# Two hybrid layers before two attention-and-experts layers on one core: small loads after the first weights, both attentions' turns side by side, four banks for the sections between

## The chip, the cores and the metric

The kernel runs on one NeuronCore of a Trainium2 chip. The metric is the device time of one execution in microseconds (us). All data is float32. Five engines work side by side: TensorE (PE, its weight loads are PEld), VectorE (DVE), ScalarE (ACT), GpSimd (POOL) and SyncE (SP), which here only issues loads. They wait for each other through semaphores, and each runs its own instructions in order.

## The reference

256 tokens of width 1024 go through two blocks of two layers each. The change touches the first block alone. One of its layers computes

```
h = rmsnorm(x);  p = h @ w_in                      # 1024 -> 3488, split in 15 parts
q = rmsnorm(cq) @ w_uq ; kv = rmsnorm(ckv) @ w_ukv # latent attention ("mla"), 4 heads of 96
q = rope(rmsnorm(q)); k = [rmsnorm(k_nope), rope(rmsnorm(kr))]
o_a = causal_attention(q, k, v_a)
o_b = c_b * short_conv(c_c * c_h)                  # 3 taps
o_c = sg_u * (tril(sg_w) @ layernorm(sg_v) + sg_b)
qd, kd = rope(rmsnorm(mq)), rope(rmsnorm(mk))      # second attention ("moba"), 4 heads of 64
o_d = causal_attention(qd, kd, mv)                 # 256 tokens are one block: plain causal
x = x + [o_a silu(g_a), o_b silu(g_b), o_c silu(g_c), o_d silu(g_d)] @ w_out
```

The second block has two layers, each an attention (neighbourhood, then grouped) and 32 experts of which each token uses two; all experts' weights are read. A vector `c` gives shifts, scales and gates of the second block through `ada_w` (1024 x 6144 for each layer).

## The kernel before

Everything stands in one program with one block per engine; the order of the work is written out by hand, engine by engine, and a result's place is found by name: `begin(b, name)` on TensorE waits until PSUM bank b is free (`drained`), `end` signals `filled`, and the engine that copies the result out signals `drained`. There are eight banks of 128 x 512.

**Weights.** They come in pieces of 1024 x 512 (2 MB), or 1024 x 416 for `cq`, into a ring of five slots, all issued by SyncE in the order of `LOADS` (line 60). A piece waits until the one that held its slot is used up. For the first layer the order is cq, qk, v, ada, s, a, ada, b, ada, g, ... Before `qk`, SyncE waits (in the first layer only) for all small loads `in` and `lay0`.

**Small loads** are issued by GpSimd at its start: five under the name `in` (positions, two gains, `c`, and 128 x 704 of constants), then `layer_loads(0)` (six, named `lay0`: gains, taps, `w_uq`, `w_ukv`, `sg_w`), then ten named `in2`. Behind them on GpSimd's queue stand the reciprocal roots that the norms wait for (line 2171): `xrs`, then, after a wait for `lay0` and four selections on `sg_w`, `rs6`, `rs8`, `rs12`, `srs`.

**A layer of the first block** (`first_layer`, on each engine its own). TensorE: 16 turns of x into columns (`xT`); the two products `cq`; the section `qk` of the first token tile; `cqT`, `ckT` turns; `qk` of the second tile; the products `q` and `kv`; then, by calls of `fill()`, the sections v0, v1, a sum `tot` of an `ada` vector, s0. A section is 16 products of 128 x 256 (32 passes in the trace). It waits for `mla` and turns the first attention's queries and keys (`hT`, 16 turns, banks 0 to 3); then section s1; then it waits for `moba` and turns the second attention's (`dT`, 8 turns, banks 0 and 1); then `attend` runs four groups of scores, softmax, turns and values, with a `fill()` (a0, a1, ...) in each round. The banks of the fills are dealt out in turn from `fill_bank`: 7 and 6 up to the attention, then 7, 2, 3. In the second layer the fill of qk1 has a `tot` too.

VectorE's fills are emptied by `settle()` in the order of `MIX_SIDE`, ScalarE's in the order of `FILL`. VectorE scales and rotates the first attention's queries and keys (tells `mla`), empties `tot` and v1, copies half of `hT`, then waits for `sq12` (ScalarE's squares of the second attention's, which ScalarE makes after `mla` and after its copies of `hT`), sums them, gets `rs12` from GpSimd, scales and rotates (tells `moba`), copies half of `dT`, and goes into `attend`.

In the names of the rows `bk` is a PSUM bank, `ring` the weight ring, `AR` the arena with nearly all activations, `st` the small statistics, `diag` the scratch of the `ada` sums. Line 425 is a turn, 429 a product, 637 a group's scores, 1009 a VectorE tensor_tensor, 2297 SyncE's load.

## Time and profile before

| | us |
|---|---|
| median of 3 runs | 1616.68 (1615.48 to 1617.62) |
| the profiled execution | 1619.63 |
| its span on the core | 1617.9 |
| TensorE matmuls busy in it | 1407.1 (87%) |
| VectorE busy | 568.5 (35%) |
| ScalarE busy | 219.3 (14%) |
| GpSimd busy | 87.9 (5%) |

The first block takes about the first 345 us of the span, the neighbourhood attention the stretch up to about 530, its experts up to about 985, and the second attention and its experts the rest. In the experts' stretches the DMA engines are nine tenths busy in every slice; in the first 345 us they are not. "PEclk" is the share of TensorE's full clock that was granted; it has two levels, 0.5 (1.2 GHz) and 1.0 (2.4 GHz). Idle time in square brackets names what ended it.

### The profile page before, as it was taken

How to read it: one execution, taken by the hardware profiler on the slowest of the kernel's cores; microseconds unless marked ns; L12 is line 12 of the kernel's file. 1: busy time of each engine (PE TensorE's matmuls, PEld its weight loads, DVE VectorE, ACT ScalarE, POOL GpSimd, SP SyncE). 2: the span in 40 equal slices, each digit the busy share in tenths (PEclk: the TensorE clock that was granted, in tenths of full speed). 3: DMA queues.
4: the chain of work that ended last, by engine and by line, in shares of the span. 5: the costliest groups of instructions: out<-in, count | busy, mean ns of one | idle time of the engine just before them, and what ended most of it. 6: DMA issues, size and time to landing. Idle time of an engine off the chain costs nothing.

```text
span 1617.9 us, 28390 instructions
## 1 busy us (share of the span) xinstructions
PE 1407.1 (87%) x12800; PEld 893.9 (55%) x12800; DVE 568.5 (35%) x1230; ACT 219.3 (14%) x578; POOL 87.9 (5%) x95
## 2 busy tenths in 40 slices
PE   6989998999899898897897887878899888887895
PEld 3776467758787554363464443447554544544542
DVE  2586557655765111011111105593411111111113
ACT  2131113202242000000000001342200000000000
POOL 3110102000002100000000000100300000000000
PEclk9999999999998999899899998989899988999999
DMA  9545853686757899999999999345799999999995
GB/s 341 199 155 200 297 204 121 240 290 235 270 198 286 350 426 426 427 426 428 428 425 427 427 387 332 117 156 217 295 426 426 426 427 427 426 427 428 426 418 203
DMA packets 96858, 533.33 MB, mean 330 GB/s; under 512 B 5185, under 2 KB 7425, under 8 KB 73169
## 3 DMA queue, kind: packets, MB, share of 16 engines
q1 hardware_dynamic: 92992, 519.40, 79.7%
q0 software_dynamic: 3728, 11.95, 2.1%
q8 instruction: 105, 1.72, 0.4%
q14 instruction: 33, 0.26, 0.0%
HBM read 530.28 MB, written 1.05 MB: 328 GB/s over the span
## 4 chain that ended last, share of the span: by engine, by line
PE 62%; DMA 25%; DVE 7%; ACT 2%; issue 1%; SPq 1%; POOL 0%; DVEq 0%; ACTq 0%
PE bk L429 24%; DMA AR<-in_moe_w_down 24%; PE bk L890 17%; PE bk L924 8%; PE bk L608 3%; PE bk L934 3%; PE bk L425 3%; DVE AR L1009 3%; ACT AR L1815 2%; PE bk L637 1%; PE bk L652 1%; SPq L2297 1%; DMA ring<-in_w_in 1%; DVE mpart L1017 1%; DMA ring<-in_ada_w 1%
## 5 line engine op out<-in xcount | busy, mean ns | idle before, releaser
L890 PE MATMUL bk<-ring,AR 128*32 128x128 f32 x5120 | 307.8, 409 | 3.8 <-DVE AR L1014 3.8
L890 PEld LDWEIGHTS bk<-ring,AR 128*32 128x32 f32 x5120 | 192.6, 127 | 102.3 <-DVE AR L1014 4.8
L429 PE MATMUL bk<-ring,AR 128*128 128x256 f32 (+2 forms) x736 | 216.3, 452 | 18.6 <-DMA ring<-in_w_in 7.1
L1009 DVE TENSOR_TENSOR AR<-bk,AR 128x128 f32<-128x128 f32 (+2 forms) x106 | 41.2, 389 | 531.6 <-ACT AR L1815 467.7
L1815 ACT ACTIVATE AR<-bk 128x512 f32<-128x512 f32 (+4 forms) x178 | 71.8, 422 | 1070.2 <-PE bk L890 789.2
L924 PE MATMUL bk<-ring,AR 128*32 128x512 f32 x656 | 161.8, 706 | 38.9 <-DMA ring<-in_moe_w_down 38.9
L429 PEld LDWEIGHTS bk<-ring,AR 128*128 128x128 f32 x736 | 142.8, 197 | 87.0 <-issue 55.5
L924 PE MATMUL bk<-AR 128*32 128x512 f32 x368 | 146.5, 704 | 48.9 <-DMA AR<-in_moe_w_down 48.1
L890 PE MATMUL bk<-AR 128*32 128x128 f32 x3072 | 187.4, 410 | 0.4 <-DMA AR<-in_moe_w_up 0.4
L429 PE MATMUL bk<-AR,ring 128*128 128x256 f32 (+1 forms) x832 | 175.4, 371 | 6.9 <-DVE diag L1009 5.5
L429 PEld LDWEIGHTS bk<-AR,ring 128*128 128x128 f32 x832 | 150.8, 194 | 28.8 <-DVE diag L1009 5.9
L890 PEld LDWEIGHTS bk<-AR 128*32 128x32 f32 x3072 | 127.9, 128 | 52.3 <-DVE X L1009 4.6
L924 PEld LDWEIGHTS bk<-AR 128*32 128x32 f32 x368 | 32.4, 127 | 147.6 <-issue 79.4
L425 PE MATMUL bk<-cst,AR 128*128 128x128 f32 (+1 forms) x356 | 67.2, 303 | 45.3 <-DVE AR L1009 31.4
L1009 DVE TENSOR_TENSOR AR<-bk,mpart 128x512 f32<-128x512 f32 x32 | 22.1, 691 | 229.4 <-PE bk L924 229.4
L1017 DVE SCALAR_TENSOR_TENSOR mpart<-ring,ccol,mpart 128x512 f32<-128x512 f32 x126 | 98.7, 783 | 4.5
L2171 POOL TENSOR_TENSOR st<-st,half 128x1 f32<-128x1 f32 (+5 forms) x24 | 33.0, 1378 | 1218.8 <-DVE st L1013 1065.8
L425 PEld LDWEIGHTS bk<-cst,AR 128*128 128x128 f32 (+1 forms) x356 | 43.6, 148 | 84.6 <-issue 54.7
L429 PE MATMUL bk<-AR 128*128 128x128 f32 (+1 forms) x536 | 72.7, 296 | 0.4 <-DVE AR L1009 0.3
L429 PEld LDWEIGHTS bk<-AR 128*128 128x128 f32 x536 | 67.6, 203 | 4.7 <-issue 2.5
L924 PEld LDWEIGHTS bk<-ring,AR 128*32 128x32 f32 x656 | 33.8, 127 | 64.1 <-DMA ring<-in_moe_w_down 53.3
L934 PE MATMUL bk<-AR 128*128 128x512 f32 x128 | 59.7, 606 | 3.3 <-DVE AR L1009 3.3
(152 smaller groups left out, 972.8 us busy)
## 6 DMA issues: line engine op xcount, KB each, us to landing
ring<-in_moe_w_gate SPq DMA_DIRECT2D x48, 2048.0 KB, 24.9
ring<-in_moe_w_down SPq DMA_DIRECT2D x36, 2048.0 KB, 28.7
ring<-in_moe_w_up SPq DMA_DIRECT2D x32, 2048.0 KB, 20.8
AR<-in_moe_w_up SPq DMA_DIRECT2D x32, 2048.0 KB, 29.4
ring<-in_ada_w SPq DMA_DIRECT2D x24, 2048.0 KB, 11.1
AR<-in_moe_w_down SPq DMA_DIRECT2D x20, 2048.0 KB, 28.6
AR<-in_moe_w_gate SPq DMA_DIRECT2D x16, 2048.0 KB, 16.7
ring<-in_w_in SPq DMA_DIRECT2D x12, 2048.0 KB, 10.5
```

The lines of the kernel that those rows point to most:

```text
L425: return eng.transpose(o, a, ident[0:k, 0:k])
L429: ins = eng.matmul(o, l, r, start=i == 0, stop=i == len(pairs) - 1)
L608: ins = eng.matmul(o[:, :], BIG[:, x, OUTS[m] + 128 * t:OUTS[m] + 128 * t + 128], w[:, 2 * m + x, :], start=k + x == 0, stop=k + x == 4)
L637: ins = eng.matmul(o[b][:, a * nk:(a + 1) * nk], g["q"][h][:, t * 128:(t + 1) * 128], g["k"][h][:, 0:nk], start=True, stop=True)
L652: ins = eng.matmul(o[64 * b:64 * b + 64, 128 * x:128 * x + 128], g["v"][2 * x + b][kt], ET[j % 2][:, (2 * b + x) * nkt + kt, :], start=kt ...
L890: ins = eng.matmul(o[32 * f:32 * f + 32, 128 * m:128 * m + 128], XG[u][:, c, 32 * j:32 * j + 32], w[:, c, f::4], start=c == 0, stop=c == N ...
L924: ins = eng.matmul(o[32 * j:32 * j + 32, :], AT[u][:, j, 32 * f:32 * f + 32], w, start=f == 0, stop=f == 3)
L934: end(eng.matmul(o[:, :], GST[u][:, 128 * t:128 * t + 128], YS[:, 512 * n:512 * n + 512], start=True, stop=True), "cb", i, q, n, t)
L1009: return eng.tensor_tensor(o, a, b, op)
L1017: return eng.scalar_tensor_tensor(out=o, in0=a, scalar=s, in1=b, op0=op0, op1=op1)
L1815: return eng.activation(o, a, f, **kw)
L2171: g.tell(eng.tensor_tensor(o, a, half[:, 0:n], ALU.pow), sem(done), value)
```

## The change

Five things are done, none of which changes what is computed.

- GpSimd waits for the landing of the first weights (`cq`, slot 0) before `layer_loads(0)` and all that stands behind; SyncE no longer waits for small loads before `qk`.
- ScalarE computes the rotation tables and silu(c) of the first layer after the squares of `cq` and no longer before them.
- ScalarE squares the second attention's queries and keys (`sq12`) right after the first one's squares; VectorE sums them beside the first one's sums and scales and rotates them right after the first one's, ahead of `tot`, v1 and the copies of `hT`.
- TensorE turns `dT` straight after `hT`; s1 comes behind both.
- v0, v1, `tot`, s0, s1 are dealt to banks 7, 5, 4, 6, 7.

```
@@ -558,6 +558,8 @@
                     end(product(o[:, 0:384], [(cqT[:, c, t * 128:(t + 1) * 128], wuq[:, c, :]) for c in range(2)]), "q", l, t)
                     o = begin(4 + t, "kv", l, t)
                     end(product(o[:, :], [(ckT[:, t * 128:(t + 1) * 128], wukv)]), "kv", l, t)
+
+                fill_bank[0] = [7, 5, 4, 6]
                 fill()
                 fill()
                 fill()
@@ -569,7 +571,6 @@
                             for t in range(NT):
                                 ins = turn(o[0:96, hh * 256 + t * 128:hh * 256 + (t + 1) * 128], src[:, t, 2 * pr + hh, :])
                         end(ins, "hT", l, i, pr)
-                fill()
                 pe.wait_ge(sem("moba"), l + 1)
                 for b, off in enumerate((MQ, MK)):
                     o = begin(b, "dT", l, b)
@@ -578,6 +579,7 @@
                             ins = turn(o[:, pr * 256 + t * 128:pr * 256 + (t + 1) * 128],
                                        BIG[:, t, off + 128 * pr:off + 128 * pr + 128])
                     end(ins, "dT", l, b)
+                fill()
                 fill_bank[0] = [7, 2, 3]
 
                 def ready(n):
@@ -1258,6 +1260,10 @@
                 v.chain()
                 v.step(ts(H8[:, :, 0:4], H8[:, :, 0:4], 1.0 / 96, ALU.mult, EPS, ALU.add))
                 v.tell(ts(H8[:, :, 4:8], H8[:, :, 4:8], 1.0 / 64, ALU.mult, EPS, ALU.add), sem("var8"), l + 1)
+                v.wait_ge(sem("sq12"), l + 1)
+                v.step(red(H12, sq1.rearrange("p t (h d) -> p t h d", d=64), ALU.add))
+                v.chain()
+                v.tell(ts(H12, H12, 1.0 / 64, ALU.mult, EPS, ALU.add), sem("var12"), l + 1)
                 krr = sect(KR, 32)
                 v.wait_ge(*drained("in", l, "cq", 0))
                 v.step(tt(krr, krr, rn(2, 32), ALU.mult))
@@ -1281,26 +1287,22 @@
                     v.step(tt(KA[:, t, :, 0:64], KA[:, t, :, 0:64], bcast(rows[:, R_KN:R_KN + 64], 1, 4), ALU.mult))
                 rope([[q4[:, t, :, 64 + 16 * i:80 + 16 * i] for i in range(2)] for t in range(NT)],
                      lambda t: bcast(cosr[:, t, 0:16], 1, 4), lambda t: bcast(sinr[:, t, 0:16], 1, 4), 4, 64, "mla")
+                x8 = [BIG[:, t, MQ:MQ + 512].rearrange("p (h d) -> p h d", h=8) for t in range(NT)]
+                v.wait_ge(sem("rs12"), l + 1)
+                for t in range(NT):
+                    v.step(tt(x8[t], x8[t], bcast(R12[:, t, :], 2, 64), ALU.mult))
+                v.chain()
+                for t in range(NT):
+                    x4 = BIG[:, t, MQ:MQ + 512].rearrange("p (k h d) -> p k h d", k=2, h=4)
+                    v.step(tt(x4, x4, bcast(rows[:, R_DQ:R_DQ + 128].rearrange("p (k d) -> p k d", k=2), 2, 4), ALU.mult))
+                rope([[x8[t][:, :, 0:8], x8[t][:, :, 8:16]] for t in range(NT)],
+                     lambda t: bcast(cosr[:, t, 16:24], 1, 8), lambda t: bcast(sinr[:, t, 16:24], 1, 8), 8, 64, "moba")
                 settle()
                 settle()
                 for i, dst in enumerate((QAT, KAT)):
                     v.wait_ge(*filled("hT", l, i, 1))
                     free(eng.tensor_copy(dst[:, 2:4, :], bank("hT", l, i, 1)[0:96, :].rearrange("p (h n) -> p h n", h=2)),
                          "hT", l, i, 1)
-                v.wait_ge(sem("sq12"), l + 1)
-                v.step(red(H12, sq1.rearrange("p t (h d) -> p t h d", d=64), ALU.add))
-                v.chain()
-                v.tell(ts(H12, H12, 1.0 / 64, ALU.mult, EPS, ALU.add), sem("var12"), l + 1)
-                x8 = [BIG[:, t, MQ:MQ + 512].rearrange("p (h d) -> p h d", h=8) for t in range(NT)]
-                v.wait_ge(sem("rs12"), l + 1)
-                for t in range(NT):
-                    v.step(tt(x8[t], x8[t], bcast(R12[:, t, :], 2, 64), ALU.mult))
-                v.chain()
-                for t in range(NT):
-                    x4 = BIG[:, t, MQ:MQ + 512].rearrange("p (k h d) -> p k h d", k=2, h=4)
-                    v.step(tt(x4, x4, bcast(rows[:, R_DQ:R_DQ + 128].rearrange("p (k d) -> p k d", k=2), 2, 4), ALU.mult))
-                rope([[x8[t][:, :, 0:8], x8[t][:, :, 8:16]] for t in range(NT)],
-                     lambda t: bcast(cosr[:, t, 16:24], 1, 8), lambda t: bcast(sinr[:, t, 16:24], 1, 8), 8, 64, "moba")
                 settle()
                 settle()
                 v.wait_ge(*filled("dT", l, 1))
@@ -1868,12 +1870,6 @@
                         s.step(ins)
                         s.chain()
                 even_columns("xT", l, ng[:, l])
-                if not l:
-                    s.wait_ge(sem("angles"), 1)
-                    s.step(act(sinr[:, :, :], view(A_SS + 96, NT, 24), ACT.Sin))
-                    s.tell(act(cosr[:, :, :], view(A_SS + 144, NT, 24), ACT.Sin), sem("tables"), 1)
-                    s.wait_ge(sem("in"), 80)
-                    s.tell(act(ccol[:, :], ccol[:, :], ACT.Silu), sem("silc"), 1)
                 s.wait_ge(*filled("in", l, "cq", 0))
                 s.wait_ge(sem("xrs"), l + 1)
                 free(act(BIG[:, 0, CQ:CQ + 416], bank("in", l, "cq", 0)[:, 0:416], ACT.Copy, scale=st2[:, 48:49]), "in", l, "cq", 0)
@@ -1886,6 +1882,12 @@
                             s.tell(ins, sem("sq6"), l + 1)
                         else:
                             s.step(ins)
+                if not l:
+                    s.wait_ge(sem("angles"), 1)
+                    s.step(act(sinr[:, :, :], view(A_SS + 96, NT, 24), ACT.Sin))
+                    s.tell(act(cosr[:, :, :], view(A_SS + 144, NT, 24), ACT.Sin), sem("tables"), 1)
+                    s.wait_ge(sem("in"), 80)
+                    s.tell(act(ccol[:, :], ccol[:, :], ACT.Silu), sem("silc"), 1)
                 settle()
                 s.wait_ge(*filled("q", l, 0))
                 free(act(QF[:, 0, :], bank("q", l, 0)[:, 0:384], ACT.Copy), "q", l, 0)
@@ -1901,20 +1903,19 @@
                         s.tell(ins, sem("sq8"), l + 1)
                     else:
                         s.step(ins)
+                for t in range(NT):
+                    s.wait_ge(*drained("in", l, "qk", t))
+                s.tell(act(sq1, sect(MQ, 512), ACT.Square), sem("sq12"), l + 1)
+                settle()
                 settle()
                 settle()
                 for i, dst in enumerate((QAT, KAT)):
                     s.wait_ge(*filled("hT", l, i, 0))
                     free(act(dst[:, 0:2, :], bank("hT", l, i, 0)[0:96, :].rearrange("p (h n) -> p h n", h=2), ACT.Copy),
                          "hT", l, i, 0)
-                for t in range(NT):
-                    s.wait_ge(*drained("in", l, "qk", t))
-                s.wait_ge(sem("mla"), l + 1)
-                s.tell(act(sq1, sect(MQ, 512), ACT.Square), sem("sq12"), l + 1)
-                settle()
-                settle()
                 s.wait_ge(*filled("dT", l, 0))
                 free(act(WA[:, 0:512], bank("dT", l, 0)[:, :], ACT.Copy), "dT", l, 0)
+                settle()
                 attend(("mix", l), settle)
                 while todo:
                     settle()
@@ -2239,6 +2240,8 @@
             small(kvg[:, :, :], A["mla_kv_norm_g"], "in")
             small(ccol[:, :], A["c"], "in")
             small(cst[:, K_TRI:K_END], A["cst"][:, K_TRI:K_END], "in")
+
+            g.wait_ge(*loaded("in", 0, "cq"))
             layer_loads(0)
             small(sgb[:, :, :], A["sg_b"], "in2")
             small(abc[:, :, :], A["ada_b_cols"], "in2")
@@ -2334,9 +2337,6 @@
                 for f in LOADS[l]:
                     if f == "cq":
                         rect(A["w_in"][l], CQ, 416, "in", l, f)
-                        if not l:
-                            sp.wait_ge(sem("in"), 80)
-                            sp.wait_ge(sem("lay0"), 96)
                     elif f == "ada":
                         ada(next(n_ada))
                     elif f in SEG:
```

The parts of the diff are, in this order, TensorE (lines 558 to 585), VectorE (1258 to 1311), ScalarE (1868 to 1925), GpSimd (2239) and SyncE (2334).

On TensorE, from section v1 of the first layer on, there stood, in this order, v1, `tot`, s0, the 16 turns `hT`, s1, the 8 turns `dT`, the first scores, a0:

```order
L429 MATMUL bk<-AR,ring 128x256 x16
L429 MATMUL bk<-mpart,ones 128x512
L429 MATMUL bk<-ring,AR 128x256 x16
L425 MATMUL bk<-cst,AR 96x128 x16
L429 MATMUL bk<-AR,ring 128x256 x16
L425 MATMUL bk<-cst,AR 128x128 x8
L637 MATMUL bk<-AR 128x128 x4
L429 MATMUL bk<-AR,ring 128x256 x16
```

and now, at the same place:

```order
L429 MATMUL bk<-AR,ring 128x256 x16
L429 MATMUL bk<-mpart,ones 128x512
L429 MATMUL bk<-ring,AR 128x256 x16
L425 MATMUL bk<-cst,AR 96x128 x16
L425 MATMUL bk<-cst,AR 128x128 x8
L429 MATMUL bk<-AR,ring 128x256 x16
L639 MATMUL bk<-AR 128x128 x4
L429 MATMUL bk<-AR,ring 128x256 x16
```

Only s1 and the 8 turns have changed places.

On VectorE, before, behind the last addition of the first attention's rotation, with what each waits for: `tot` and v1 were emptied, two of `hT` copied, and then the second attention's sums and scaling began:

```order
L1009 TENSOR_TENSOR AR<-AR 128x4x16 x3
L1009 TENSOR_TENSOR diag<-bk,cst 64x512 [waits s_filled7,s_in2]
L1020 TENSOR_REDUCE dsum<-diag 64x8 [waits s_drained7]
L1009 TENSOR_TENSOR AR<-bk,AR 128x2x256 [waits s_v,s_filled6]
L1288 COPY AR<-bk 96x512 [waits s_filled1]
L1288 COPY AR<-bk 96x512 [waits s_filled3]
L1020 TENSOR_REDUCE st<-AR 128x16 [waits s_sq12]
L1014 TENSOR_SCALAR st<-st 128x16 [waits s_v]
L1009 TENSOR_TENSOR AR<-AR,st 128x512 [waits s_rs12]
```

and now:

```order
L1011 TENSOR_TENSOR AR<-AR 128x4x16 x3
L1011 TENSOR_TENSOR AR<-AR,st 128x512 [waits s_rs12]
...
L1011 TENSOR_TENSOR AR<-AR 128x8x8 x3
L1011 TENSOR_TENSOR diag<-bk,cst 64x512 [waits s_filled4,s_in2]
L1022 TENSOR_REDUCE dsum<-diag 64x8 [waits s_drained4]
L1011 TENSOR_TENSOR AR<-bk,AR 128x2x256 [waits s_v,s_filled5]
L1304 COPY AR<-bk 96x512 [waits s_filled1]
```

The scaling and rotation of the second attention (to `128x8x8 x3`) stand ahead of the emptying of `tot` and v1; the sum that waits for `sq12` stands further up.

## Rows read from the trace of the kernel before

**Rows 1.** timeline of TensorE's matmuls, first layer: start us, busy us, line, [idle before <-releaser].

```profile
17.74 20.00 PE L429 MATMUL bk<-ring,AR 128*128 128x416 f32 x48 [7.08 <-DMA ring<-in_w_in]
...
63.67 1.02 PE L429 MATMUL bk<-mpart,ones 128*128 128x512 f32 x2
67.42 7.17 PE L429 MATMUL bk<-ring,AR 128*128 128x256 f32 x32 [2.73 <-DVE AR L1009]
74.44 1.91 PE L425 MATMUL bk<-cst,AR 128*96 128x128 f32 x16
76.18 7.07 PE L429 MATMUL bk<-AR,ring 128*128 128x256 f32 x32
86.50 1.97 PE L425 MATMUL bk<-cst,AR 128*128 128x128 f32 x8 [3.25 <-DVE AR L1009]
...
98.67 1.06 PE L637 MATMUL bk<-AR 96*128 96x128 f32 x8
99.56 7.07 PE L429 MATMUL bk<-AR,ring 128*128 128x256 f32 x32
...
126.60 1.09 PE L425 MATMUL bk<-cst,AR 128*128 128x128 f32 x8
```

**Rows 2.** the same view in the second layer, and one gap of the third stage.

```profile
214.32 7.07 PE L429 MATMUL bk<-ring,AR 128*128 128x256 f32 x32
...
228.13 1.02 PE L429 MATMUL bk<-mpart,ones 128*128 128x512 f32 x2
...
265.21 1.06 PE L637 MATMUL bk<-AR 96*128 96x128 f32 x8
...
347.37 14.05 PE L429 MATMUL bk<-AR,ring 128*128 128x256 f32 x64 [1.41 <-DVE AR L1014]
```

**Rows 3.** timeline of the sync engine's queue, start: issue us, time of the issues, target.

```profile
2.19 14.95 SPq L2297 DMA_DIRECT2D ring<-in_w_in  x3
```

**Rows 4.** DMA by queue and by load (us from issue to landing), first 7 us, first 60 us.

```profile
q1 hardware_dynamic: 666, 1.30, 55.3%
...
ring<-in_w_in SPq DMA_DIRECT2D x1, 1664.0 KB, 15.5
...
AR<-in_sg_w POOLq DMA_DIRECT2D x1, 256.0 KB, 8.7
```

**Rows 5.** stretches: PE, PEld, DVE, ACT, POOL busy us (count), PEclk, DMA share, GB/s.

```profile
18.00:20.00 2.00, 2.00 (x4) 0.92 (x5) 0.00 (x0) 0.00 (x0) 0.00 (x0) 0.50 0.97 365
20.00:40.00 20.00, 20.00 (x58) 10.47 (x57) 3.99 (x11) 3.32 (x14) 1.34 (x1) 0.97 1.05 389
```

**Rows 6.** timeline of GpSimd (POOL), start of the kernel.

```profile
12.31 0.54 POOL L2174 DMA_DIRECT2D qkn<-in_gqa_qk_norm  x1
...
15.87 1.03 POOL L2215 TENSOR_SCALAR_AFFINE_SELECT AR<-AR 128x128 f32<-128x128 f32 x4 [2.18 <-DMA AR<-in_sg_w]
32.90 1.34 POOL L2171 TENSOR_TENSOR st<-st,half 128x6 f32<-128x6 f32 x1 [16.00 <-DVE st L1013]
```

**Rows 7.** timeline of VectorE (DVE), first layer.

```profile
10.70 0.88 DVE L1013 TENSOR_SCALAR AR<-bk,ng 128x256 f32<-128x256 f32 x2 [0.83 <-PE bk L425]
...
61.47 0.63 DVE L1009 TENSOR_TENSOR AR<-AR 128x64 f32<-128x64 f32 x4
...
66.68 0.69 DVE L1009 TENSOR_TENSOR AR<-bk,AR 128x512 f32<-128x512 f32 x1
...
81.96 1.29 DVE L1009 TENSOR_TENSOR AR<-AR,st 128x512 f32<-128x512 f32 x2 [3.01 <-POOL st L2171]
...
85.82 0.63 DVE L1009 TENSOR_TENSOR AR<-AR 128x64 f32<-128x64 f32 x4
...
89.30 0.69 DVE L1009 TENSOR_TENSOR AR<-bk,AR 128x512 f32<-128x512 f32 x1
...
98.87 0.69 DVE L1009 TENSOR_TENSOR AR<-bk,AR 128x512 f32<-128x512 f32 x1 [2.72 <-PE bk L429]
```

**Rows 8.** timeline of VectorE (DVE), second layer.

```profile
215.13 0.67 DVE L1009 TENSOR_TENSOR diag<-bk,cst 64x512 f32<-64x512 f32 x1
```

More of the change, by code:

```diff
@@ L571, in first_layer @@
                         end(ins, "hT", l, i, pr)
-                fill()
                 pe.wait_ge(sem("moba"), l + 1)
@@ L580, in first_layer @@
                     end(ins, "dT", l, b)
+                fill()
                 fill_bank[0] = [7, 2, 3]
@@ L1260, in first_layer @@
                 v.tell(ts(H8[:, :, 4:8], H8[:, :, 4:8], 1.0 / 64, ALU.mult, EPS, ALU.add), sem("var8"), l + 1)
+                v.wait_ge(sem("sq12"), l + 1)
+                v.step(red(H12, sq1.rearrange("p t (h d) -> p t h d", d=64), ALU.add))
+                v.chain()
+                v.tell(ts(H12, H12, 1.0 / 64, ALU.mult, EPS, ALU.add), sem("var12"), l + 1)
                 krr = sect(KR, 32)
@@ L1283, in first_layer @@
                      lambda t: bcast(cosr[:, t, 0:16], 1, 4), lambda t: bcast(sinr[:, t, 0:16], 1, 4), 4, 64, "mla")
-                settle()
-                settle()
-                for i, dst in enumerate((QAT, KAT)):
-                    v.wait_ge(*filled("hT", l, i, 1))
-                    free(eng.tensor_copy(dst[:, 2:4, :], bank("hT", l, i, 1)[0:96, :].rearrange("p (h n) -> p h n", h=2)),
-                         "hT", l, i, 1)
-                v.wait_ge(sem("sq12"), l + 1)
-                v.step(red(H12, sq1.rearrange("p t (h d) -> p t h d", d=64), ALU.add))
-                v.chain()
-                v.tell(ts(H12, H12, 1.0 / 64, ALU.mult, EPS, ALU.add), sem("var12"), l + 1)
                 x8 = [BIG[:, t, MQ:MQ + 512].rearrange("p (h d) -> p h d", h=8) for t in range(NT)]
@@ L1303, in first_layer @@
                      lambda t: bcast(cosr[:, t, 16:24], 1, 8), lambda t: bcast(sinr[:, t, 16:24], 1, 8), 8, 64, "moba")
+                settle()
+                settle()
+                for i, dst in enumerate((QAT, KAT)):
+                    v.wait_ge(*filled("hT", l, i, 1))
+                    free(eng.tensor_copy(dst[:, 2:4, :], bank("hT", l, i, 1)[0:96, :].rearrange("p (h n) -> p h n", h=2)),
+                         "hT", l, i, 1)
                 settle()
@@ L1870, in first_layer @@
                 even_columns("xT", l, ng[:, l])
-                if not l:
-                    s.wait_ge(sem("angles"), 1)
-                    s.step(act(sinr[:, :, :], view(A_SS + 96, NT, 24), ACT.Sin))
-                    s.tell(act(cosr[:, :, :], view(A_SS + 144, NT, 24), ACT.Sin), sem("tables"), 1)
-                    s.wait_ge(sem("in"), 80)
-                    s.tell(act(ccol[:, :], ccol[:, :], ACT.Silu), sem("silc"), 1)
                 s.wait_ge(*filled("in", l, "cq", 0))
@@ L1888, in first_layer @@
                             s.step(ins)
+                if not l:
+                    s.wait_ge(sem("angles"), 1)
+                    s.step(act(sinr[:, :, :], view(A_SS + 96, NT, 24), ACT.Sin))
+                    s.tell(act(cosr[:, :, :], view(A_SS + 144, NT, 24), ACT.Sin), sem("tables"), 1)
+                    s.wait_ge(sem("in"), 80)
+                    s.tell(act(ccol[:, :], ccol[:, :], ACT.Silu), sem("silc"), 1)
                 settle()
@@ L1903, in first_layer @@
                         s.step(ins)
+                for t in range(NT):
+                    s.wait_ge(*drained("in", l, "qk", t))
+                s.tell(act(sq1, sect(MQ, 512), ACT.Square), sem("sq12"), l + 1)
+                settle()
                 settle()
@@ L1909, in first_layer @@
                          "hT", l, i, 0)
-                for t in range(NT):
-                    s.wait_ge(*drained("in", l, "qk", t))
-                s.wait_ge(sem("mla"), l + 1)
-                s.tell(act(sq1, sect(MQ, 512), ACT.Square), sem("sq12"), l + 1)
-                settle()
-                settle()
                 s.wait_ge(*filled("dT", l, 0))
                 free(act(WA[:, 0:512], bank("dT", l, 0)[:, :], ACT.Copy), "dT", l, 0)
+                settle()
                 attend(("mix", l), settle)
@@ L2241, in _ @@
             small(cst[:, K_TRI:K_END], A["cst"][:, K_TRI:K_END], "in")
+            g.wait_ge(*loaded("in", 0, "cq"))
             layer_loads(0)
@@ L2336, in _ @@
                         rect(A["w_in"][l], CQ, 416, "in", l, f)
-                        if not l:
-                            sp.wait_ge(sem("in"), 80)
-                            sp.wait_ge(sem("lay0"), 96)
                     elif f == "ada":
```

1 line of the change is left out of this document (added).

## The prediction

> **What bounds the kernel now.** I read the page's shares first, then the chain that ended last, then TensorE's timeline. In the two expert stages the weights' DMA is the limit and nothing here touches it. But the loads of a stage start when TensorE or VectorE frees a slot, so what the first 345 us lose or gain moves everything behind by the same amount. In those 345 us TensorE works almost without a break; the question is which breaks the change closes. [rows 1] show them in the first layer: 7.08 us before the first product, until `cq` has landed; 2.73 us before s0, until VectorE has emptied bank 6 (v1); 3.25 us before `dT`, until VectorE has scaled and rotated the second attention. The second layer has the last two again, between its `tot` and its second scores [rows 2].
>
> **Part A, the start.** SyncE issues `cq` at 2.19 [rows 3], and it lands 15.5 us later, at 17.7, since GpSimd's small loads run beside it [rows 4]. By 7.0 us SyncE's queue had moved 1.30 MB [rows 4]. Up to the end of `cq` it has 64 + 8 + 1024 + 1664 KB, 2.83 MB, so 1.53 MB are left; the five loads `in`, which stay ahead, add 0.36 MB (128 x 704 words). At 389 GB/s [rows 5] these 1.89 MB take 4.9 us: landing at 11.9. Without the small ones it would be 10.9, but then VectorE's last column section counts, done at 10.70 + 0.88 = 11.6 [rows 7]. If the small ones take half of the engines until they land (about 10 us), it is 12.6. I take 11.9 and get 17.74 - 11.9 = **5.8 us** (5.1 to 6.1).
>
> TensorE's clock adds to that. After the idle 7.08 us the first product ran at 0.5 [rows 5]. The mean of 0.97 over the next 20 us says half a clock until about 21.2, so 3.45 us at half speed, 1.7 us lost. In the new order the idle time ahead is 11.9 - 10.66 = 1.3 us. The one lone gap of that size before the third stage's sections, 1.41 us [rows 2], was followed by 64 passes in 14.05 us, the full rate, while 7.08 and 3.25 us were followed by half speed (the 8 turns at 86.50 took 1.97 us, at 126.60 only 1.09). So I count the **1.7 us** as gained; at the low end they are not.
>
> What is late next? GpSimd waits for `cq`, then issues 16 small loads at 0.54 us [rows 6], and only then computes `xrs` at 20.7 to 21.5. The first 48 passes took 20.0 us with 1.7 lost [rows 1]; less the last 16 (section qk, 7.0) the two `cq` products need 11.3, so they end at 17.6 and 23.2. `xrs` is late for ScalarE's copy of the first, but the chain goes on with the second: hidden. Then GpSimd waits for `lay0`: its six loads are issued by 15.5 and the last takes 8.7 us [rows 4], 24.2; selections 1.03, 25.2; `rs6` is asked for at 32.90 - 5.8 - 1.7 = 25.4 and takes 1.34 [rows 6]. TensorE needs it for `cqT` only after section qk, 7 us behind the second product, at 30.2; `rs6` and VectorE's scaling end at 28. Slack 2 us. `qk` itself follows `cq` on SyncE's queue: 2.1 MB and the small loads' 1.8 MB at 389 are 10 us, so it lands before 22 and is asked for at 23.2. `ada`, `s` and `a` have more room. ScalarE's tables and silu(c) move behind the squares of `cq`, into a time in which ScalarE has nothing to do until section qk ends at 30.2; VectorE asks for them only after `cqT`. Hidden.
>
> A rule that speaks to this part: the Trainium skill, page "DMA: Bandwidth & Descriptors", section "Queues, rings and completion order", says that each DMA engine takes turns between the queues it has work for, packet by packet. By that rule small loads behind a full SyncE queue get their turn (this trace agrees so far as `sg_w` took 8.7 us beside `cq`), and the sum stays; without it the first rival below holds.
>
> **Part B, from the end of `tot` to the second scores, first layer.** Before, `tot` ends at 63.67 + 1.02 = 64.69 and the second scores start at 98.67 [rows 1]: 33.98 us. Now v1 stands in bank 5 and s0 in bank 6, which has long been empty, so s0 starts at 64.69. A section at full clock takes 7.02 us (67.42 to 74.44), `hT` 1.74 (74.44 to 76.18), `dT` 1.09 (126.60), the first scores 0.89 (98.67 to 99.56). s0 + `hT` + `dT` + s1 + scores + a0 = 3 x 7.02 + 1.74 + 1.09 + 0.89 = 24.8 us. **Gain 9.2 us.** In it are the two waits (6.0); the rest, 3.2, is the half clock behind the second of them and a short wait of the scores for the copies of `dT`.
>
> This asks that `moba` be there when `hT` ends, at 64.69 + 8.8 = 73.5. VectorE ended the first rotation at 61.47 + 0.63 = 62.1 [rows 7]. It now takes the sums of `sq12` along (1.4 us, partly under the wait for `rs8`), then the scaling and rotation, 81.96 to 86.45, 4.5 us; at the most 62.1 + 1.4 + 4.5 = 68.0. Slack 5 us. `rs12` takes GpSimd 3.0 us (the 3.01 of idle time at 81.96) and is asked for before the first scaling, so it is there before the rotation ends. `tot` and v1 are emptied after 68, but their banks 4 and 5 are wanted by nobody before the values and turns of `attend`. The copies of `hT` are needed in banks 0 and 1 by `dT` and follow within 0.7 us of each half, as before.
>
> Does VectorE then hold up the rounds, where it is busy nearly all the time? Before, from emptying s1 at 89.30 it reached 96.15, and waited 2.72 us for a0 [rows 7]: 6.85 us of work. Now TensorE leaves it 0.89 + 7.02 = 7.9 us between the end of s1 and that of a0. It still waits for a0, with 1 us to spare, and everything behind a0 keeps its distances. a0 goes into bank 7 right after s1, which VectorE has emptied 0.75 us later, under the scores' 0.89: no wait, or 0.1.
>
> **Part B, second layer.** Before: 229.15 (228.13 + 1.02) to 265.21, 36.06 us [rows 2]; now the same 24.8: gain 11.3. But there is a new wait. qk1's fill has a `tot` there, which stood in bank 7 and which VectorE empties at 215.13 to 215.80 [rows 8]. Section v0 started at 214.32 [rows 2] in bank 6; it is now dealt bank 7 and must wait until 215.8: **1.5 us**. Queued behind v0 is all of TensorE; VectorE and ScalarE have work. A lone gap of that size cost no clock above. Gain 11.3 - 1.5 = **9.8 us** (8.1 if the clock falls).
>
> **The sum.** 5.8 + 1.7 + 9.2 + 9.8 = 26.5 us. The profiled execution took 1619.63 and would take 1593.1; it lies 2.95 above the median of 1616.68, so the median should be 1590.2. The other gaps' half-clock phases shift with the time at which they come; each is worth 1.7 us either way, which I take as 3 us.
>
> **Rivals.** (1) Small loads starve. If SyncE's queue, now never empty at the start, keeps the engines to itself, `lay0` lands only when `cq` and five pieces are through, 11.9 + 5 x 5.4 = 39, and its own 4.6 us later, 43.5. Then `cqT` stands at about 47 and not 30: 17 us and 1.7 of clock back, 1609. Against it: `sg_w`'s 8.7 us beside a busy queue [rows 4], and [rows 6], where it ended the wait at 15.87, before `cq`. 5%. It bites from a landing later than 26.
>
> (2) The start gives less: `cq` lands at 12.6 or later, and the half clock falls all the same; 2.4 us less, 1592.6, or up to 1595 together with a clock loss in the second layer. 20%.
>
> (3) Part of B is given back in the rounds: VectorE's 1 us to spare is used up (its `ada` pieces come later, GpSimd's `rs` slows it), and it becomes the bound of the first rounds, 2 to 4 us in each layer: 1594 to 1598. For it: it has no other free time there. Against: the 2.72 us of waiting [rows 7]. 12%.
>
> (4) Slower. TensorE now has next to no breaks in 260 us. If a long unbroken stretch is itself granted half a clock now and then, each such piece costs 1.7 us in 3.4, and from 16 of them on the kernel is slower: 20 would give 1624. The place is the sections of both layers. Against it: 20 to 40 us, all of it busy, has 0.97, and what is missing is the start's [rows 5]. With anything that I do not see, 2%.
>
> (5) It does not do what it says: SyncE's queue shares its engines among its own loads, so that `cq` lands with `qk` behind it no sooner than before. Then A is nought: 1597.7. 3%.
>
> **How the numbers follow.** Forecast 1590.2 (1585 to 1594), 58%; rivals 20, 12, 5, 3 and 2%. The range from 1585 to 1599 takes in (2), (3) and (5). A measurement of this kernel can tell about 0.2%, 3.2 us, from no change: faster needs less than 1613.4, which all but (4) and a grave form of (1) give. Faster 0.95, same 0.03, slower 0.02.
>
> **What would show it.** In the new trace: TensorE's first product near 12 and at full clock; `cqT` right behind qk0; s0 right behind `tot`; `hT`, `dT`, s1 without idle time; VectorE still waiting for a0 in each layer; 1.5 us of idle time ahead of v0 in the second layer; everything from the neighbourhood stage on earlier by the same 26 us. The forecast is wrong if `lay0` lands after 26 us, if VectorE has no wait left at a0, or if the later stages do not move along.

## The result, and the profile after

The changed kernel takes **1588.55 us** (median of 4 runs, 1588.30 to 1592.42), the one before 1616.70 us beside it: the ratio is 0.983, 95% interval 0.9815 to 0.9849. The forecast was 1590.2 us. Its profiled execution took 1588.65 us (span 1586.9 us), against 1619.63 us (span 1617.9 us) for the profiled one of before.

The first view is TensorE's timeline in the first layer (start us, busy us, line, operation, tiles and shapes, count, [idle before <-releaser]), as in [rows 1]:

```profile
12.59 18.31 PE L429 MATMUL bk<-ring,AR 128*128 128x416 f32 x48 [1.75 <-DMA ring<-in_w_in]
30.73 0.59 PE L429 MATMUL bk<-diag,ones 128*128 128x256 f32 x2
...
56.83 1.02 PE L429 MATMUL bk<-mpart,ones 128*128 128x512 f32 x2
57.68 7.07 PE L429 MATMUL bk<-ring,AR 128*128 128x256 f32 x32
64.59 2.78 PE L425 MATMUL bk<-cst,AR 128*96 128x128 f32 x24
67.21 7.07 PE L429 MATMUL bk<-AR,ring 128*128 128x256 f32 x32
...
82.08 1.06 PE L639 MATMUL bk<-AR 96*128 96x128 f32 x8
```

Three brackets of [rows 1] are gone or small: 7.08 became 1.75, and the 2.73 ahead of s0 and the 3.25 ahead of `dT` are no more. The 24 turns at 64.59 are `hT` and `dT` in one group. Second scores: 98.67 before, 82.08 now.

The same view in the second layer, to set beside [rows 2]:

```profile
164.78 18.28 PE L429 MATMUL bk<-ring,AR 128*128 128x416 f32 x48 [1.98 <-ACT AR L1817]
182.90 0.59 PE L429 MATMUL bk<-diag,ones 128*128 128x256 f32 x2
...
190.88 1.02 PE L429 MATMUL bk<-mpart,ones 128*128 128x512 f32 x2
191.74 4.46 PE L429 MATMUL bk<-AR 128*128 128x384 f32 x12
197.57 7.17 PE L429 MATMUL bk<-ring,AR 128*128 128x256 f32 x32 [1.37 <-DVE diag L1011]
...
211.49 1.02 PE L429 MATMUL bk<-mpart,ones 128*128 128x512 f32 x2
...
236.74 1.06 PE L639 MATMUL bk<-AR 96*128 96x128 f32 x8
```

The forecast new wait is there: v0 stands 1.37 us until VectorE has emptied `diag`'s bank.

How far TensorE is ahead of before, read at the same instruction in both timelines, tells where the time came from:

| TensorE's mark | before | after | ahead |
|---|---|---|---|
| first `cq` product | 17.74 | 12.59 | 5.2 |
| `tot`, first layer | 63.67 | 56.83 | 6.8 |
| second scores, first layer | 98.67 | 82.08 | 16.6 |
| first `cq` product, second layer | 181.37 | 164.78 | 16.6 |
| `tot` of `qk1` | 209.16 | 190.88 | 18.3 |
| `tot` behind v1 | 228.13 | 211.49 | 16.6 |
| second scores, second layer | 265.21 | 236.74 | 28.5 |
| sections of the third stage | 347.37 | 318.89 | 28.5 |
| end of the span | 1617.9 | 1586.9 | 31.0 |

So the start gave 6.8 us, the first layer's middle 9.75, the second's 11.8 less 1.6 for v0's wait, and 1.7 came between the two `cq` products of the second layer and its `tot`. Behind the third stage's first sections the lead still moves by 2.5 us, without an edit that would explain it. Where it can be followed it is the clock (the turns and scores at 457.98 and 459.81 us of before take 1.90 and 1.96 us, the same ones of after 1.09 and 1.13) and landing times of weights. That belongs to these two executions: the profiled one of before lies 2.9 us over its median and that of after 0.1.

At the start, the issue times of SyncE and GpSimd and the landings show what was reordered. SyncE's queue timeline, GpSimd's timeline (two pieces), and loads by landing time (count, KB each, us from issue to landing):

```profile
2.19 7.00 SPq L2300 DMA_DIRECT2D ring<-in_w_in  x3
```

```profile
12.82 1.06 POOL L2175 DMA_DIRECT2D AR<-in_rows  x2 [8.64 <-DMA ring<-in_w_in]
...
23.92 1.03 POOL L2216 TENSOR_SCALAR_AFFINE_SELECT AR<-AR 128x128 f32<-128x128 f32 x4 [1.58 <-DMA AR<-in_sg_w]
26.05 1.34 POOL L2172 TENSOR_TENSOR st<-st,half 128x6 f32<-128x6 f32 x1 [1.10 <-DVE st L1015]
```

```profile
ring<-in_w_in SPq DMA_DIRECT2D x1, 1664.0 KB, 10.4
...
AR<-in_sg_w POOLq DMA_DIRECT2D x1, 256.0 KB, 8.1
```

`cq` lands 10.4 us after its issue and not 15.5 [rows 4]; `sg_w`, issued at 15.79 beside a SyncE queue that is never empty, still lands in 8.1 us, so `lay0` is there by 23.92. VectorE in the rounds (its timeline; the wait for s1, then that for a0):

```profile
74.32 0.69 DVE L1011 TENSOR_TENSOR AR<-bk,AR 128x512 f32<-128x512 f32 x1 [6.22 <-PE bk L429]
...
82.28 0.69 DVE L1011 TENSOR_TENSOR AR<-bk,AR 128x512 f32<-128x512 f32 x1 [1.12 <-PE bk L429]
```

It still waits 1.12 us for a0, where it had 2.72 [rows 7].

### The profile page after: what moved, and what is told of

Its sections match the earlier page's. It is cut to its first block, busy times and chain, and to the rows that moved or that the text cites. A ratio compares the mean times of both kernels' runs of the same rounds, so it can differ in the third digit from the quotient of the medians.

```text
span 1586.9 us, 28389 instructions
## 1 busy us (share of the span) xinstructions
PE 1397.0 (88%) x12800; PEld 885.6 (56%) x12800; DVE 568.5 (36%) x1230; ACT 219.4 (14%) x578; POOL 87.9 (6%) x95
## 4 chain that ended last, share of the span: by engine, by line
PE 64%; DMA 25%; DVE 7%; ACT 2%; issue 1%; SPq 1%; DVEq 0%; ACTq 0%
PE bk L429 25%; DMA AR<-in_moe_w_down 24%; PE bk L892 18%; PE bk L926 8%; PE bk L610 3%; PE bk L936 3%; PE bk L425 3%; DVE AR L1011 2%; ACT AR L1817 1%; PE bk L654 1%; PE bk L639 1%; DVE mpart L1019 1%; SPq L2300 1%; DMA ring<-in_w_in 1%; DMA ring<-in_ada_w 1%
## 5 line engine op out<-in xcount | busy, mean ns | idle before, releaser
L429 PE MATMUL bk<-ring,AR 128*128 128x256 f32 (+2 forms) x736 | 211.7, 445 | 9.0 <-DVE lsum L1011 3.0
```

The lines of the kernel that those rows point to most:

```text
L429: ins = eng.matmul(o, l, r, start=i == 0, stop=i == len(pairs) - 1)
```

## The experiments

Twelve kernels, four at a time beside runs of the kernel before. None leaves out a part of the computation; those with dummy products add some that nobody reads. "Fewer than before" is against the median beside them (1617.63, 1616.55 or 1618.49 us).

**The halves of the change.** `e1_start_only` is the kernel before with part A (GpSimd waits for `cq`, SyncE's two waits go, ScalarE's tables move behind the squares):

```diff
             small(cst[:, K_TRI:K_END], A["cst"][:, K_TRI:K_END], "in")
+            g.wait_ge(*loaded("in", 0, "cq"))
             layer_loads(0)
...
                         rect(A["w_in"][l], CQ, 416, "in", l, f)
-                        if not l:
-                            sp.wait_ge(sem("in"), 80)
-                            sp.wait_ge(sem("lay0"), 96)
```

> The kernel before with the start of the changed one alone: GpSimd's small loads behind cq, SyncE's queue free, ScalarE's tables behind the squares. My theory (the two parts are independent, and the start is worth the earlier landing plus the half clock: 17.74 - 12.59 = 5.15 and 1.7 us): 1616.7 - 6.9 = 1609.8 us, with 1.7 us either way from the phase of the clock at later gaps. Rival (the parts need each other: GpSimd and VectorE give it back where the old order waits): above 1613.

Measured: 1610.92 us (7 runs), 6.7 fewer; ratio 0.9958 (0.9944 to 0.9972), about 1 us above the expected time and within its 1.7 us. TensorE's timeline has the new start and both old gaps:

```profile
12.46 18.31 PE L429 MATMUL bk<-ring,AR 128*128 128x416 f32 x48 [1.66 <-DMA ring<-in_w_in]
...
60.46 7.17 PE L429 MATMUL bk<-ring,AR 128*128 128x256 f32 x32 [2.73 <-DVE AR L1009]
...
79.54 1.97 PE L425 MATMUL bk<-cst,AR 128*128 128x128 f32 x8 [3.25 <-DVE AR L1009]
```

`e2_middle_only` is the changed kernel with these edits, and the move of ScalarE's tables, taken back.

> The changed kernel with the start of the one before: the turns of both attentions side by side and the four banks alone. Theory: the first layer's middle is worth 9.8 us, the second's 10.2, and 1.7 the clock between the layers: 1616.7 - 20 = 1596.7, or 1595 with the clock. Rival (the start's part makes room for the middle's): 1600 or more.

Measured: 1598.53 us (4 runs), 19.1 fewer; 0.9886 (0.9869 to 0.9904). That is 1.8 us above the expected 1596.7 and below the rival's 1600. The halves make 25.8 us, the whole 28.2. In the profiled executions the marks tell what is missing: at the third stage's turns the halves lead by 6.8 and 18.7 us and the whole by 28.5. Of these 3.0 us, 1.7 is the second layer's `cq` products (half clock in e2 as in before, full in the profile after), and 1.2 is e2's own start, where the first products begin 0.2 us later and take 21.02 us, in before 20.00. So nearly all of it is TensorE's rate in single executions, and no tie between the halves is left to look for in them; that the medians' 2.4 us have the same origin is likely and not shown.

**The banks.** `e4_banks_only` is the kernel before with the one line that deals four banks in the rounds:

```diff
+                fill_bank[0] = [7, 5, 4, 6]
                 fill()
```

> The kernel before with the four banks alone, order untouched. Theory: s0 no longer waits for v1 to be emptied (2.73 us in the first layer, 2.88 and 1.8 of half clock in the second), v0 of the second layer waits 1.5 us, and the 3.25 us ahead of the second attention's turns stay in both: 1616.7 - 2.7 - 3.2 = 1610.8. Rival (the banks are what frees everything, the order of the turns matters little): below 1603. Other rival (the 3.25 us grow by what is saved, since the squares wait for the first turns' copies): 1616.

Measured: 1611.38 us (7 runs), 6.3 fewer; 0.9956 (0.9942 to 0.997), as expected. TensorE's timeline: s0 has no idle time any more, the 3.25 us ahead of `dT` stay.

```profile
66.05 7.07 PE L429 MATMUL bk<-ring,AR 128*128 128x256 f32 x32
...
85.03 1.56 PE L425 MATMUL bk<-cst,AR 128*128 128x128 f32 x8 [3.25 <-DVE AR L1011]
```

`e5_two_banks` is the changed kernel without that line.

> The changed kernel with the old two banks (7 and 6) for the sections. Theory: VectorE now empties v1 only after the second attention's rotation (62.4 us in the changed kernel's trace), and s0 in the same bank waits for it from 57.8 on: 4.6 us in the first layer, as much in the second, each with up to 1.7 of half clock, less the 1.5 us of v0's wait in the second: 1588.5 + 7.7 to 11.1 = 1596 to 1600. Rival (the order of the turns alone gives the gain, the banks do little): below 1591.

Measured: 1603.18 us (4 runs), 13.4 fewer; 0.9911 (0.9894 to 0.9928), above the expected 1596 to 1600. TensorE's timeline in the two layers (the second row is cut at 232 us, where the stretch asked for ends), and windows (us; PE, PEld, DVE, ACT, POOL busy with counts, PEclk, DMA share, GB/s) behind the first gap:

```profile
64.12 9.34 PE L429 MATMUL bk<-ring,AR 128*128 128x256 f32 x32 [4.56 <-DVE AR L1010]
...
226.81 5.49 PE L429 MATMUL bk<-ring,AR 128*128 128x256 f32 x12 [5.53 <-DVE AR L1010]
```

```profile
66.00:68.00 2.00, 2.00 (x6) 1.64 (x5) 0.00 (x0) 0.00 (x0) 0.00 (x0) 0.50 1.05 387
68.00:70.00 2.00, 2.00 (x9) 1.67 (x9) 0.00 (x0) 0.00 (x0) 0.00 (x0) 0.87 1.05 385
```

Turning the second attention early without more banks puts VectorE's scaling and rotation ahead of the emptying of v1's bank, and s0's wait grows from 2.73 to 4.56 us (5.53 in the second layer). Behind each gap the clock stands at 0.50 (in the second layer too, from 227 to 231 us), and the sections take 9.34 and 9.91 us where they took 7.07: 2.3 and 2.8 us on top of the idle time. The expectation had at most 1.7 for each and 4.6 us of idle time in both layers, which is why it came out too low. The four banks are worth 6 us alone and nearly 15 under the new order (1603.18 against 1588.55).

**A third order of the banks.** `e3_banks_6547` changes one line of the changed kernel, so that v0 gets bank 6, not the bank of `tot`:

```diff
-                fill_bank[0] = [7, 5, 4, 6]
+                fill_bank[0] = [6, 5, 4, 7]
```

> The changed kernel with the banks dealt 6, 5, 4, 7 and not 7, 5, 4, 6, so that v0 of the second layer does not wait for VectorE to empty the ada sum in bank 7. Theory: the 1.37 us of idle time ahead of v0 at 196.2 goes (1.5 us with the queueing), and nothing else changes: 1.5 us faster than the changed kernel, 1587.0. Rival (VectorE or a weight sets the rounds behind it and takes it back): 1588.5, with the idle time at another place of the second layer.

Measured: 1588.50 us (1586.74 to 1591.22, 4 runs); 0.982 (0.9798 to 0.9842). The median is that of the changed kernel and not the expected 1587.0, but the interval is over 3 us wide on either side and leaves room for 1.5 us. It is the rival's number without the rival's reason, since no idle time appears elsewhere in the second layer. TensorE's timeline has v0 without idle time, and the stretch from the first layer's `tot` to the third stage's turns is 256.6 us instead of 258.6. What it won there its profiled execution lost at the start, where the first products took 19.82 us instead of 18.31:

```profile
12.59 19.82 PE L429 MATMUL bk<-ring,AR 128*128 128x416 f32 x48 [1.74 <-DMA ring<-in_w_in]
...
193.05 4.46 PE L429 MATMUL bk<-AR 128*128 128x384 f32 x12
197.35 7.07 PE L429 MATMUL bk<-ring,AR 128*128 128x256 f32 x32
```

**The parts of the start.** `e6_small_loads_first` takes GpSimd's wait for `cq` out of the changed kernel, `e7_sync_waits` puts SyncE's two waits back into it, `e8_tables_early` puts ScalarE's tables and silu(c) back ahead of its copy of `cq`.

```diff
e6:
-            g.wait_ge(*loaded("in", 0, "cq"))
             layer_loads(0)
e7:
                         rect(A["w_in"][l], CQ, 416, "in", l, f)
+                        if not l:
+                            sp.wait_ge(sem("in"), 80)
+                            sp.wait_ge(sem("lay0"), 96)
e8:
                 even_columns("xT", l, ng[:, l])
+                if not l:
+                    s.wait_ge(sem("angles"), 1)
...
+                    s.tell(act(ccol[:, :], ccol[:, :], ACT.Silu), sem("silc"), 1)
                 s.wait_ge(*filled("in", l, "cq", 0))
```

> The changed kernel with GpSimd's small loads issued at once, as before; SyncE's queue stays free. Theory: the small loads beside cq are what made it land late, so cq lands near 17.7 again, the first product starts there at half clock and the start's 6.9 us are lost: 1595.4. Rival (the gain comes from SyncE's queue being free): 1589.

> The changed kernel with SyncE waiting again for the small loads before qk; GpSimd's still come behind cq. Theory: lay0 lands at 23.9, qk is issued there and lands 8.3 us later at 32.2, and TensorE wants it at 23.9: 8.3 us idle and up to 3.4 of half clock, 1588.5 + 8.3 + 1.7 = 1598.5 (1597 to 1600). Rival (qk has room, the freed queue is worth nothing): 1589.

> The changed kernel with ScalarE's rotation tables and silu(c) again ahead of its copy of cq. Theory: they wait for VectorE's angles at 16.1 and end near 18.0, while the copy waits for xrs until 22.4 in any case: no change, 1588.5. Rival (ScalarE's order is part of the start's gain): 1590 or more, with cqT later.

Measured: e6 1597.62 us (4 runs; 0.9876, 0.986 to 0.9893), e7 1600.18 us (4 runs; 0.9899, 0.9883 to 0.9916), e8 1588.36 us (4 runs; 0.9822, 0.9806 to 0.9839). TensorE's timeline of e6, then of e7:

```profile
18.06 20.92 PE L429 MATMUL bk<-ring,AR 128*128 128x416 f32 x48 [7.28 <-DMA ring<-in_w_in]
```

```profile
12.45 13.48 PE L429 MATMUL bk<-ring,AR 128*128 128x416 f32 x32 [1.67 <-DMA ring<-in_w_in]
31.44 9.89 PE L429 MATMUL bk<-ring,AR 128*128 128x512 f32 x16 [5.52 <-DMA ring<-in_w_in]
```

And SyncE's queue in e7:

```profile
2.19 20.45 SPq L2300 DMA_DIRECT2D ring<-in_w_in  x3
```

Both times lie some 2 us above their expectations (1595.4, and 1598.5 with 1597 to 1600), that of e8 on it. GpSimd's small loads are what holds `cq` up: without their wait the first product starts at 18.06. And with SyncE's waits for `lay0` behind GpSimd's, `qk` is issued late: TensorE stands 5.52 us before section qk and then works at half clock for a part (9.89 us where the changed kernel needs 7.0), which gives back what the early `cq` won. Each edit without the other (1597.6 and 1600.2 us) is no better than neither (e2, 1598.5, in another round); together they are worth some 10 us. ScalarE's tables cost nothing in either place.

**The clock at the gaps.** `e9_changed_again` is the changed kernel once more. `e10_kept_busy` has TensorE multiply `ones` into bank 7 while it waits: twelve products ahead of X's turns, fourteen (`busy(7)`) behind them, ahead of `cq`.

```diff
+            def busy(n):
+                for _ in range(n):
+                    eng.matmul(banks[7][:, 0:128], ones[:, :], ones[:, :], start=True, stop=True)
+                    eng.matmul(banks[7][:, 128:256], ones[:, :], ones[:, :], start=True, stop=True)
...
                 columns(X, "xT", l)
+                if not l:
+                    busy(7)
```

> The changed kernel itself once more, beside the next three on the same chip. Theory (whether TensorE's clock is at half when cq lands differs from one execution to the next: its first product ended at 30.7 in one trace, at 32.2 to 32.5 in three others of the same start): single times in two groups 1.7 to 3.4 us apart, median 1588 to 1591. Rival (the half clock falls by the kernel's order): one group within 1 us of 1588.5.

> The changed kernel with TensorE kept at work at the start by products of ones into bank 7 that nobody reads: 12 before the column turns, 14 behind them. Theory: the clock is full when cq lands in every execution, the first product starts at 12.6 and its 48 passes take 18.3 us, and the single times lose their upper group: median 1588, 1 us below the changed kernel's beside it. Rival (the clock does not matter here, the groups come from later gaps): the same times and spread as the changed kernel, or slower if the extra products stand in the way of the turns.

Measured, 5 runs each: e9 1589.74 us (1588.47 to 1590.44; 0.9825, 0.9811 to 0.9839), e10 1589.63 us (1586.97 to 1590.63; 0.9821, 0.9806 to 0.9836). The times of e9 (1588.47, 1589.07, 1589.74, 1590.27, 1590.44) don't fall into the two groups that were expected, and e10 isn't the expected 1 us faster: keeping TensorE busy changed nothing that can be told here. TensorE's timeline of e9 in the second layer, one row; it is the same kernel as the one profiled above, with the same 1.98 us of idle time, and took 19.97 us where that took 18.28:

```profile
164.75 19.97 PE L429 MATMUL bk<-ring,AR 128*128 128x416 f32 x48 [1.98 <-ACT AR L1817]
```

The windows over the first 2 us of this group (PEclk is the third number from the end), e9 first, then the profile after:

```profile
165.00:167.00 2.00, 2.00 (x4) 0.93 (x4) 1.93 (x3) 0.00 (x0) 1.10 (x1) 0.50 0.79 213
```

```profile
165.00:167.00 2.00, 2.00 (x7) 1.04 (x7) 1.93 (x3) 0.00 (x0) 1.14 (x1) 1.00 1.00 240
```

The start of e10 has 0.25 us of idle time and full clock. But `cq` lands as in e9 (12.54), whose first products happened to run at full clock as well, so nothing starts or ends sooner.

```profile
12.51 18.31 PE L429 MATMUL bk<-ring,AR 128*128 128x416 f32 x48 [0.25 <-DMA ring<-in_w_in]
```

Its dummy products show at what clock an execution starts: two passes take 0.63 us at first and 0.39 later, and the trace's record of the clock opens between them, at 5.16 us, with a rise to full. In e12 it opens at 6.99.

```profile
2.16 0.63 PE L470 MATMUL bk<-ones 128*128 128x128 f32 x2
...
5.38 0.39 PE L470 MATMUL bk<-ones 128*128 128x128 f32 x2
```

**The rest of the start, and all together.** `e11_banks_constants` has the banks of e3 and moves the largest load of `in` behind GpSimd's wait; `e12_all_three` is e11 with the dummy products of e10.

```diff
-            small(cst[:, K_TRI:K_END], A["cst"][:, K_TRI:K_END], "in")
-
             g.wait_ge(*loaded("in", 0, "cq"))
+            small(cst[:, K_TRI:K_END], A["cst"][:, K_TRI:K_END], "in")
             layer_loads(0)
```

> The changed kernel with banks 6, 5, 4, 7 and with the 0.36 MB of constants moved behind cq as well. Theory: v0's 1.4 us in the second layer go, and cq lands 0.9 us sooner (0.36 MB at 389 GB/s), near 11.8, where VectorE's column section ends: 2.3 us below the changed kernel beside it, 1586 to 1587. Rival (the angles, which wait for the constants, now come at 24 and hold VectorE's copy of cq, and with it cqT): 1588 or more, with idle time ahead of cqT.

> The last two together: banks 6, 5, 4, 7, constants behind cq, TensorE kept at work at the start. Theory: 1.4 + 0.9 + about 1 us below the changed kernel beside it: 1585.5 to 1586.5, in one group. Rival: no better than the one before it.

Measured, 5 runs each: e11 1588.46 us (1587.99 to 1591.07; 0.982, 0.9805 to 0.9835), e12 **1586.91 us** (1584.26 to 1588.46; 0.9807, 0.9791 to 0.9823). e12 is the fastest of all and 2.8 us under e9 beside it, whose runs (from 1588.47) all lie above its own (up to 1588.46); that is near the bound of what can be told. e11 is 1.3 us under e9 where 2.3 was expected, and e12 1.55 under e11, with runs that overlap: what the dummy products add to e11 is not shown. TensorE's first group in e11, then in e12:

```profile
11.85 20.29 PE L429 MATMUL bk<-ring,AR 128*128 128x416 f32 x48 [1.06 <-DVE AR L1015]
```

```profile
12.22 18.20 PE L429 MATMUL bk<-ring,AR 128*128 128x416 f32 x48
```

In e11 the releaser is now VectorE's last column section and not the DMA, as the prediction said for a `cq` without small loads beside it; but the group's products passed in part at half the rate. In e12 it starts 0.4 later, behind the dummy products, and runs at full rate. At the third stage's turns e12 is at 312.92, 2.5 us ahead of the profile after: 0.5 from the start, 2.0 from the banks. This profile is of e12's fastest run.

## Why the prediction was right

**Part A, landing of `cq`.** Forecast 11.9, measured 12.59: 5.2 us and not 5.8, at the low end of the range. The rate was right, 396 GB/s from 7.0 to 12.5. What the sum left out is the end of a load. Counting bytes (SyncE's queue q1: packets, MB, share), e7 shows it, as SyncE there issues `qk` only after its wait for the small loads, so that nothing follows `cq`. The first line is e7's first 12.0 us, the second the changed kernel's first 12.5 us:

```profile
q1 hardware_dynamic: 1600, 2.83, 63.3%
```

```profile
q1 hardware_dynamic: 1749, 3.13, 67.7%
```

In e7 the queue's traffic thins out from 11.4 on, the 2.83 MB are through at 12.0, and the first product starts at 12.45. So the last engines end some 0.5 us behind the first, and 0.45 to 0.65 us lie between the last packets and the product. In the changed kernel the queue has by 12.5 moved 0.30 MB of `qk` as well, which reads as if engines that are through went on to it. It costs `cq` nothing that can be told: the same start is at 12.42 to 12.60 in the profiles that have `qk` behind it. That the forecast's other case (small loads on half of the engines) said 12.6 is luck. Its own figures give 12.4, and the small loads moved no more than their 0.37 MB.

**Part A, the clock.** The 1.7 us were there in the profile after (18.31 us for 48 passes, against 20.00), so the number held, but by luck: the reasoning failed. It asked whether a gap of 1.3 us makes the clock fall, and took one lone gap of 1.41 us as proof that it doesn't. What decides in most profiles is when the clock first rises. All fourteen profiled executions start at half clock: X's 16 turns take 3.5 to 3.7 us, and only in e10 and e12, behind the dummy products, 2.05. Of the eight profiles in which `cq` comes early and TensorE is not kept busy, three (after, e1, e9) have the record of the clock open with the rise at 10.74 to 11.34 us, before `cq` lands, and their first products run at full clock. In four (e3, e7, e8, e11) it opens only at 15.67 to 16.59, and the first products are still at the start's half clock, which no gap brought about. Only in e5 did the clock rise (10.51) and fall again (13.92) behind the gap. Ahead of the record's opening PEclk reads 1.00 whatever the clock, so that the half clock is to be read there from the number of products. The first 2 us of the group in e3, then in the profile after:

```profile
12.60:14.60 2.00, 2.00 (x3) 1.17 (x4) 1.76 (x8) 0.00 (x0) 1.77 (x3) 1.00 1.05 408
```

```profile
12.60:14.60 2.00, 2.00 (x6) 1.20 (x7) 1.76 (x8) 0.00 (x0) 1.78 (x3) 1.00 1.04 398
```

The late start has the same draw. In before and e4 the clock had risen and fallen again; in e2 and e6 it rose only at 23.4, and there and in e4 the first products took 20.92 to 21.34 us. So the late start lost 1.7 to 3.0 us (2.5 on average over four profiles) and the early one nothing to 2.0 (1.1 over eight). An estimate from these is that the term is worth some 1.4 us on average, and in a single pair of executions anything from about nothing to 3.0: it should have stood in the sum as a range, not as "gained". Of rival (2) one half came, the landing at 12.6; the other half, the clock, came in five of the eight profiles and not in the one that was scored.

**Part A, what comes late next.** GpSimd's selections ended at 24.95 and it then waited 1.10 us for VectorE, where the forecast's times (25.2, asked for at 25.4) left it 0.2. `rs6` and VectorE's scaling ended at 28.45, and the products behind section qk started at 30.73; 28 and 30.2 were forecast. `cqT` followed without idle time, and `qk` landed in time. The starvation rival (1) fell: `sg_w` took 8.1 us. By the turn-taking of queues that the Trainium skill states (page "DMA: Bandwidth & Descriptors", section "Queues, rings and completion order") small loads get their turn beside a full queue, and the trace agrees. Rival (5) fell with 12.59, and with e7, where `cq` alone on its queue starts the products at 12.45.

**Part B, first layer.** 9.2 forecast, 9.75 measured. The missing half us: s0 starts 0.17 us before the modelled end of `tot`, the 24 turns take 2.62 us and not 2.83, and the sections follow each other at 6.9 to 7.0 us; the sum added ends. `moba` was rotated at 59.86, 6.5 us ahead of `hT`'s end, with 5 forecast. e4 and e5 show that both edits are needed for it: s0's wait stays without the banks, and `dT`'s without the new order.

**Part B, second layer.** 11.3 forecast, 11.8 measured; v0's new wait 1.5 forecast, 1.64 later in the marks (1.37 idle). e3 took it away and won these 1.6 us, with 0.2 in each layer between `tot` and the sections behind a0, where the forecast had a0 wait for bank 7 by nothing or 0.1.

**VectorE in the rounds.** 1 us to spare was forecast, 1.12 measured in the first layer and 1.11 in the second, so rival (3) did not come. Rival (4) neither: in the profile after no row of the long sections runs at half clock.

**The sum.** 26.5 forecast; 28.5 at the third stage's sections. The 2.0 between them: +1.1 in the two middles, -0.1 in v0's wait, -0.7 at the start, and +1.7 from the `cq` products of the second layer, which ran at full clock in this execution. That last one is among the phases for which the text allowed 3 us either way, and e9 shows it without: its profile leads by 26.8. The medians differ by 28.2 us here and by 28.8 beside e9.

Left open: why e3, e11 and the changed kernel have the same median although the banks of e3 and e11 take 2.0 us out of the timeline behind the first layer's `tot`. With four or five runs that spread over 3 to 4 us, a gain of 2 us can hide. Their profiled executions lost 1.5 and 2.0 us at the start by the clock (19.82 and 20.29 us for 18.31), e11's another 1.7 at the second layer's `cq` products; whether most of their other executions did too, no trace shows.

## What to carry to other kernels

Where a wait moves a load to the front of the line, look for every other wait that counts on the loads put back: here the edits of GpSimd's wait and of SyncE's were worth 7 to 10 us together and nothing singly. When an order is changed so that an engine empties a bank later, deal the banks for the new order at the same time; the same line was worth 6 us under the old one and nearly 15 under the new. Read gains from marks at the same instruction in both traces, and keep what TensorE's clock gives in a column of its own: at the start and behind short gaps it belongs to the execution, not to the kernel. When the granted clock reads 1.00 at the head of a trace, count the products before believing it.

## What the runs showed of the hardware

TensorE starts at half clock, and when it first rises differs between executions of the same start: at 10.7 to 11.3 us in some profiles of the early start and at 15.7 to 16.6 in others, which costs the first products up to 2.0 us. The record of the granted clock opens with that rise and reads 1.00 before it; the number of products in a stretch tells the clock there (3 in 2 us against 6).

The clock at one and the same gap is not fixed either. The 1.98 us of idle time at the head of the second layer stand in all profiles (1.96 to 1.98); behind it the `cq` products ran in part at 1.2 GHz in nine of fourteen (19.97 us) and at 2.4 GHz throughout in five (18.28 us), and the changed kernel itself showed both. The gap of 1.4 us at the head of the third stage never cost anything in these profiles. Gaps of 4.6 to 5.5 us in e5 and e7 each cost 2.3 to 2.9 us beyond themselves, as the section behind them ran at half clock in large part.

Dummy products in the start's waits brought the rise forward to 5.16 and 6.99 us in the two kernels that had them, ahead of X's columns (16 turns in 2.05 us, not 3.68), and the clock stayed up. No run shows that they shorten the kernel: alone they changed nothing (e10 against e9), and beside a sooner load the 1.55 us between e12 and e11 lie within the spread.

A load of 1664 KB with nothing behind it on its queue (e7) thins out over its last 0.5 us, and what waits for it starts 0.45 to 0.65 us behind its last packets. With another load behind it the start is the same (12.42 to 12.60 us against 12.45).
